# Moving the second latent pair's attention, gate, convolution and norm of layer 0 behind the first pair's router

## The reference

```
for l in range(2):
    hl, hc = modulated rmsnorm of latent and context tokens
    z = h @ w_in[l]        # q, k, v | mLSTM qk, v, o, gates | conv bg, cg, xv | 3 merge gates
    da = differential attention (latent queries see context + latent keys; context sees context)
    ml = mLSTM, both directions, chunks of 128 tokens
    cv = bg * conv3(cg * xv, w)                     # conv3 reaches one token to each side
    x += g1 * ((sig(gate0)*(da@w_da) + sig(gate1)*(ml@w_ml) + sig(gate2)*(cv@w_cv)) @ w_o)
    h = modulated rmsnorm(x)
    # PEER: 8 heads, each picks 16 of 16384 experts per token
    expert, gate = router(h)                        # 128 experts per token
    x += g2 * sum_k gate_k * gelu(u_tab[expert_k] . h) * v_tab[expert_k]
out = rmsnorm(latent x)
```

## Time and profile before

| | us |
|---|---|
| median of 3 runs | 5941.26 (5933.55 to 5946.65) |
| the profiled execution, whole | 5949.21 |
| its span | 5947.1 |
| b, from its first to c1's first matmul (762.2 to 1967.0) | 1204.8 |
| c1, to unit 3's last group (1967.0 to 2894.8) | 927.8 |
| c2, to d's first matmul (2894.8 to 3635.1) | 740.3 |
| e1, to unit 7's last group (4288.8 to 5260.7) | 971.9 |

### The profile page before, as it was taken

How to read it: one execution, slowest core, us unless ns; L and a number is a source line. 1 busy time by engine, 2 the same in 40 slices (tenths; PEclk the granted TensorE clock), 3 DMA queues, 4 the chain that set the end, 5 groups by cost and what they waited for, 6 DMA issues and landing times.

```text
span 5947.1 us, 63889 instructions
## 1 busy us (share of the span) xinstructions
PE 4117.5 (69%) x22248; PEld 2506.1 (42%) x22248; DVE 2900.9 (49%) x6835; ACT 1697.3 (29%) x4733; POOL 1441.5 (24%) x1295
## 2 busy tenths in 40 slices
PE   3889477889886685548476677778468785545555
PEld 1677454566563443224132235677335453211111
DVE  0321747544438544664445444322854445654444
ACT  0200137332432342233322222201152442222222
POOL 0000022212221232223343341000023332235443
PEclk7779789969997897778788888669778898767777
DMA  6434367748886798679999995024378997689998
GB/s 257 151 130 162 121 248 281 290 170 319 329 343 234 302 420 328 266 274 386 379 409 411 394 420 200 27 67 155 117 286 361 369 402 318 256 335 421 407 417 358
DMA packets 259315, 1712.65 MB, mean 288 GB/s; under 512 B 37712, under 2 KB 39344, under 8 KB 71600
## 3 DMA queue, kind: packets, MB, share of 16 engines
q0 software_dynamic: 184320, 1342.26, 56.4%
q1 hardware_dynamic: 74672, 366.31, 16.6%
HBM read 1690.43 MB, written 17.92 MB: 287 GB/s over the span
## 4 chain that ended last, share of the span: by engine, by line
PE 42%; DMA 24%; DVE 15%; ACT 6%; issue 4%; DVEq 4%; POOL 3%; ACTq 2%; SPq 1%; PEldq 0%; PEld 0%; POOLq 0%
PE psum L423 25%; DMA arena<-in_uv,arena 21%; PE psum L774 10%; DVE arena L2020 3%; POOL arena L1108 3%; DVE arena L1932 1%; DVE arena L1925 1%; DMA arena<-in_w_ada 1%; DVE arena L1926 1%; PE psum L383 1%; PE psum L604 1%; PE psum L605 1%; ACT arena L1444 1%; ACT arena L1441 1%; PE psum L639 1%
## 5 line engine op out<-in xcount | busy, mean ns | idle before, releaser
L1108 POOL DMA_INDIRECT arena<-in_uv,arena x1280 | 1437.6, 1123 | 4469.9 <-PE psum L774 3039.1
L774 PE MATMUL psum<-arena 64*64 64x512 f32 x10240 | 1564.5, 742 | 1086.5 <-ACTq L1445 990.9
L2020 DVE CUSTOM_DVE_ANT_0 arena<-arena 128x1024 f32<-128x1024 f32 x1280 | 1552.5, 1226 | 1330.0 <-DMA arena<-in_uv,arena 1272.4
L423 PE MATMUL psum<-arena 128*128 128x256 f32 (+2 forms) x8480 | 1945.9, 388 | 171.4 <-DVEq L1464 120.4
L423 PEld LDWEIGHTS psum<-arena 128*128 128x128 f32 (+1 forms) x8480 | 1616.9, 195 | 599.2 <-issue 194.1
L774 PEld LDWEIGHTS psum<-arena 64*64 64x64 f32 x10240 | 392.7, 157 | 2068.6 <-ACTq L1445 1375.8
L1438 ACT ACTIVATE arena<-arena 128x2 f32<-128x2 f32 x640 | 130.9, 205 | 1684.8 <-DVEq L2022 1671.3
L1444 ACT ACTIVATE arena<-arena 128x64 f32<-128x64 f32 x1280 | 376.2, 340 | 45.8 <-issue 1.8
L383 PE MATMUL psum<-arena 128*128 128x128 f32 (+1 forms) x680 | 129.4, 346 | 337.3 <-DVE arena L1523 119.8
L1441 ACT ACTIVATE arena<-arena 128x1 f32<-128x1 f32 x1280 | 307.6, 287 | 45.5 <-issue 1.3
L383 PEld LDWEIGHTS psum<-arena 128*128 128x128 f32 (+1 forms) x680 | 97.9, 178 | 391.2 <-issue 183.5
(11 more groups left out here) (210 smaller groups left out, 2747.4 us busy)
## 6 DMA issues: line engine op xcount, KB each, us to landing
arena<-in_w_in SPq DMA_DIRECT2D x92, 1024.0 KB, 5.9
arena<-in_w_mix SPq DMA_DIRECT2D x120, 768.0 KB, 7.3
arena<-in_w_ada SPq DMA_DIRECT2D x32, 1536.0 KB, 16.4
arena<-in_w_wq SPq DMA_DIRECT2D x40, 1152.0 KB, 6.0
arena<-in_w_wo SPq DMA_DIRECT2D x20, 1024.0 KB, 7.5
arena<-in_uv,arena POOLq DMA_INDIRECT x1280, 10.8
arena<-ada_rows SPq DMA_DIRECT2D x15, 512.0 KB, 5.6
arena<-x_rows SPq DMA_DIRECT2D x14, 512.0 KB, 6.2
```

The source lines that it names most:

```text
L423: ins = mm(out, a, b, start=(i == 0), stop=(i == last))
L774: ins = mm(psum[o, r_ * 512:r_ * 512 + 512], DIAG[rows, c, :], RING[rows, sl, D + half * 512:D + (half + 1) * 512], start=first, stop=last ...
L1108: pool.indirect_dma_start(RING[:, sl, :], None, io["uv"], bass.IndirectOffsetOnAxis(IDX[:, t, h * TOPK + k:h * TOPK + k + 1], 0)).then_inc ...
L2020: V_.tensor_tensor_reduce(out=RING[:, sl, 0:D], in0=RING[:, sl, 0:D], in1=XT[:, u % 2, :], scale=1.0, scalar=0.0, op0=ALU.mult, op1=ALU.ad ...
```

## The change

Segment b keeps `q`, `da` and `mc`, `mln` of pair 1 alone. Pair 2's `q`, `da`, `mc`, `mln` go to the head of c1, ahead of its `merge` and `route`. The four context stages of layer 1 go from c1 to the head of c2. b, c1 and c2 keep their numbers of groups, so the groups are spread anew over the steps.

What follows from it in the code: K^T and V (2 x 1.5 MB) are stored to DRAM (`kv_rows`) by SP at the head of `da` of pair 1, and loaded again at the first step of `q` of pair 2; ACT and DVE wait for the store at the head of `mlp`, and PE waits for the load ahead of pair 2's first scores. The weight chunks of `q` (2) and of `mc` (8) are loaded twice. Pair 1's convolution now goes ahead of pair 2's, so in its `mc` PE also multiplies the `cg` and `xv` chunks with pair 2's first column (64 matmuls of width 1, 128 instructions in the profile), and DVE finishes the last column from them. Some places in SBUF change.

```diff
-    b = [(k, 0, both) for k in ("norm1", "qkv", "da", "mlp", "ml", "mc", "mln")] + [("merge", 0, (1,)), ("route", 0, (1,))]
-    c1 = [("merge", 0, (2,)), ("route", 0, (2,))] + [(k, 1, (0,)) for k in ("norm1", "kv", "mlp", "ml")]
-    c2 = [(k, 1, (1,)) for k in ("norm1", "qkv", "mlp", "mc")]
+    b = [("norm1", 0, both), ("q", 0, (1,)), ("kv", 0, both), ("da", 0, (1,)), ("mlp", 0, both), ("ml", 0, both)] + [(k, 0, (1,)) for k in ("mc", "mln", "merge", "route")]
+    c1 = [(k, 0, (2,)) for k in ("q", "da", "mc", "mln", "merge", "route")]
+    c2 = [(k, 1, (0,)) for k in ("norm1", "kv", "mlp", "ml")] + [(k, 1, (1,)) for k in ("norm1", "qkv", "mlp", "mc")]
...
+                if (l, pairs) == (0, (2,)):
+                    pe.wait_ge(s("kv_in"), 32)
                 scores(0)
...
+                        if (l, pairs) == (0, (1,)) and name != "bg":
+                            after = buf(l, 2, "HT", [KD, PW])
+                            for i in range(2):
+                                (b,) = fill(("edge", l, name, 2 * hh + i))
+                                full(chain(bank(b, 1), [(w[:, k, i * P:(i + 1) * P], after[:, k, 0:1]) for k in range(KD)]))
...
+                        if (kind, l, pairs, n) == ("q", 0, (2,), 0):
+                            sp.wait_ge(s("kv_out"), 32)
+                            for i, a in enumerate((4096, 7168)):
+                                sp.dma_start(view(DN + a, [3072]), kv_rows[i]).then_inc(s("kv_in"), 16)
...
+                if (l, pairs) == (0, (1,)):
+                    for i, a in enumerate((4096, 7168)):
+                        sp.dma_start(kv_rows[i], view(DN + a, [3072])).then_inc(s("kv_out"), 16)
...
+                if (l, pairs) == (0, (1, 2)):
+                    dve.wait_ge(s("kv_out"), 32)
...
+                                if joined:
+                                    after = EDGE[:, m:m + 1]
+                                    (b,) = whole(("edge", l, "xv", m))
+                                    empty(TT(after, after, bank(b, 1), ALU.mult), b)
+                                    dve.drain()
+                                    conv_edge(cvt(p)[:, m, PW - 1:PW], HALO[:, 8 + m, :], after, CVCW[:, l, m, :])
```

More of the change, by code:

```diff
@@ L197, in build @@
         x_rows = nc.dram_tensor("x_rows", [TOK, D], fp32).ap()
+        kv_rows = nc.dram_tensor("kv_rows", [2, P, 3072], fp32).ap()
         def sem(name):
@@ L287, in build @@
                          RA=12288, RSM=14336, RW=8192),
-            (0, 2): dict(HT=2048, QT=11264, MLT=6144, MLV=9216, MLO=15872, CVT=7168, YMT=5120, YD=16384, YM=13312, G16=14080, STGQ=13312, STGK=15360,
-                         ROPE=16384, XS=12288, JUNK=14336, HST=15360, STAGE=12288, ROWS=14848, TEMPS=15360,
-                         COL=17920, CVS=16896, MT=8192, JUNK2=17408, SIG=12288, XS2=14336, G1=16384, RA=12288, RSM=14336, RW=8192),
+            (0, 2): dict(HT=2048, QT=10240, MLT=6144, MLV=9216, MLO=15872, CVT=7168, YMT=5120, YD=16384, YM=11264, G16=14080, STGQ=13312, STGK=15360,
+                         ROPE=0, XS=12288, JUNK=14336, HST=15360, E=12288, WM=13824, WT=14592, SQD=12288, STAGE=12288,
+                         SQM=8192, CVS=16896, NRD=18944, NRM=18944, MT=8192, JUNK2=17408, SIG=12288, XS2=14336, G1=16384, RA=12288, RSM=14336, RW=8192),
             (1, 0): dict(HT=2048, STGK=12288, XS=12288, JUNK=14336, HST=15360, MLT=15360, MLV=17408, STAGE=12288, G16=13824, ROWS=10240,
@@ L680, in edge @@
                     for i in range(2):
-                        (b,) = fill(("edge", name, 2 * hh + i))
+                        (b,) = fill(("edge", l, name, 2 * hh + i))
                         full(chain(bank(b, 1), [(w[:, k, i * P:(i + 1) * P], ht[:, k, 0:1]) for k in range(KD)]))
@@ L896, in qkv @@
             def qkv(kind, l, pairs):
-                for op in qkv_ops(kind):
+                for n, op in enumerate(qkv_ops(kind)):
                     for p in pairs:
@@ L1223, in mlp @@
             def mlp(kind, l, pairs):
+                if (l, pairs) == (0, (1, 2)):
+                    act.wait_ge(s("kv_out"), 32)
                 for p in pairs:
@@ L1529, in qkv @@
             def qkv(kind, l, pairs):
-                rope_at = DN + (1024 if kind == "q" else PLACE[l, pairs[0]].get("ROPE", 0))
+                rope_at = DN + (1024 if (kind, pairs) == ("q", (2,)) else PLACE[l, pairs[0]].get("ROPE", 0))
                 prods = [view(rope_at + 256 * i, [2 * H, 2, 16]) for i in range(4)]
@@ L1803, in mc @@
             def mc(kind, l, pairs):
+                joined = (l, pairs) == (0, (1,))
                 for c in range(2):
@@ L1821, in mc @@
                                 dve.drain().then_inc(s("cv_done"), 1)
+                                if joined:
[4 more added lines that the diff above has]
+                                    conv_edge(cvt(p)[:, m, PW - 1:PW], HALO[:, 8 + m, :], after, CVCW[:, l, m, :])
+                                    dve.drain()
+                            elif name == "cg" and joined:
+                                (b,) = whole(("edge", l, "cg", m))
+                                empty(V_.tensor_copy(EDGE[:, m:m + 1], bank(b, 1)), b)
                             elif name == "bg":
@@ L1824, in mc @@
                                 x = cvt(p)[:, m, :]
-                                if p == 1:
+                                if p == 1 and not joined:
                                     V_.tensor_copy(HBG[:, m:m + 1], bank(b)[:, PW - 1:PW])
@@ L1841, in edge @@
                         m = 2 * hh + i
-                        (b,) = whole(("edge", name, m))
+                        (b,) = whole(("edge", l, name, m))
                         e = EDGE[:, m:m + 1]
```

## The result

| | us |
|---|---|
| before, median of 8 runs | 5940.33 (5930.58 to 5949.73) |
| after, median of 8 runs | 5967.24 (5959.3 to 5980.9) |
| ratio, with its 95% interval | 1.0044 [1.0033, 1.0054] |
| span of the profiled execution, before and after | 5947.1, 5975.2 |

What follows compares the result with a forecast made beforehand. No one engine was taken to bound the kernel throughout: PE sets b's pace, gathers c2's, c1 lies between. Terms b -52, c1 +23, c2 +42 sum to +13 on 5941.3, forecast 5954 us, range 5905 to 6003.

Steps and rivals of the forecast that it cites:

- b: -52 forecast: Segment b as a whole: stages moved out, less the groups spread anew, were to shorten it by 52 us.
- priced at 27 by a row at half the clock: In `mc` of b: 128 width-1 instructions at 0.21 us each, taken from `edge`, 27.5 us with nothing hiding them.
- The third group's price of 10 us a head: In `route` of b: a third group delays the next head's scores; two heads pay 10 us each.
- The last head with 3 groups was given 5: In `route` of b: the last head with a third group pays only that group's own work, 5 us.
- e1 was the right row: For c1: e1 has nearly the stages c1 is to get; its 971.9 us was the base for c1's +23.
- the reload: At the head of c1: loading 3.1 MB delays unit 2's activations and what queues behind them, +5 us (bounds 0 and 16).
- half of one kind and half of the other: In c2: midway between +24 (bytes at 393 GB/s) and +59 (whole at 376 GB/s), giving 782 us, +42.
- the stretches taken as unchanged: Segments a, d, e1 and the end were to stay as they are, adding nothing to the sum.
- the gathers hide all of it: Rival, c1 and c2: moved steps fill idle transfer time, c1 stays at 928, c2 pays bytes; -28, 5913 us; chance 0.25.
- The two sides cancel: Rival, whole kernel: c2 pays bytes alone, c1 and b as forecast; -5, 5936 us; chance 0.17.
- The width-1 matmuls hide: Rival, `mc` of b: they hide in the groups' waits, the sum without its 27; -14, 5927 us; chance 0.05.
- the stops add up: Rival, c1 and c2: reload holds PE and stops gathers, c2's short stages run at 376 GB/s; +47, 5988 us; chance 0.13.

Runs made afterwards that it cites:

- route_two: The kernel after, with router cost 9.6 instead of 12 for pair 1 in layer 0, so every head has 2 groups: 5930.52 us, ratio 0.9983.
- no_width1: The kernel after, without the width-1 matmuls in pair 1's `mc` and the small VectorE operations that wait for them: 5949.41 us, ratio 1.0012.
- ctx_small_chunks: The kernel after, with the 8 weight chunks of the context's stages in c2 loaded at a sixteenth of their size: 5960.71 us, ratio 1.0037.

## Why the prediction was right, and where it was off

The sign and the mechanism held: b pays back less than was taken out of it, and the two stretches behind it don't take the work for nothing.

- b: -52 forecast, -50 measured. Of its stages, five came within 3 us of their forecast: `q` and `kv` 117 (117), `merge` 250.5 (252), `mln` 5.9 (about 9), `ml` 167.3 (169), `mc` 122.9 (123.5). `mlp` was 6 shorter than forecast, its 3 new groups cost next to nothing (142.5 for 142.0); `da` was 8 longer (92.8 for 85). Why, no run asks.
- `mc` was right by luck: two errors cancelled. The width-1 instructions were priced at 27 by a row at half the clock; they take 15. In turn the rest of the stage was priced 8 too low: 103.6 without them, not 96. The prediction says that the trace disagrees with the Trainium skill's page "TensorE: Matmul & The Clock Gate", section "LDWEIGHTS" (107 ns for 128 columns). At the full clock it agrees, 108 ns each. The loads fill the same time as the matmuls in the earlier trace rows, which points to the weight load as what is left at a width of 1. That such an instruction costs what one of width 256 does was wrong too: the one price was at half speed, the other at full speed.
- `route`: 229.2 for 224 forecast. The third group's price of 10 us a head is what route_two measured. The last head with 3 groups was given 5; the stage as a whole grew by 30 for its three.
- c1: +23 forecast, +21 measured; e1 was the right row, and the reload cost about the 5 us given to it.
- c2 is the term that was mis-sized: +42 forecast, +62 measured, 3 above even its upper bound. The prediction took the middle between the bytes' time at 393 GB/s and the rate of the context's stretch, 376. The step that failed is "half of one kind and half of the other". Pair 1's half did not keep its 393: it ran at 372, below the context's 383. One cause is shown. The change gave the 8 lead groups to the context's norm, and pair 1's got the stop of 24 us, which the row of c2 before does not have. Putting a lead back is worth 13 to 24 us.
- In all +27 for +13: 20 us too low in c2, less 5 from the stretches taken as unchanged. The forecast of the whole was about half of the loss.
- The rivals: "the gathers hide all of it" is out, as c1 is 949 long and not below 935. "The two sides cancel" had c2 at its bytes alone, +24. "The width-1 matmuls hide" is out by no_width1's 18 us. Of "the stops add up" half came true: c2's part (+59), but not the wait for the reload.

## What to carry to other kernels

Price a moved piece by what is spread around it anew: here the groups left behind in b took back about half of what the moved stages freed (`merge` +19 and `route` +30 among them), and a change of a cost table by one number was worth 37 us. Where an engine's stream has work that lags by a fixed number of items, count how many are handed out between two steps of a latency chain; one above the lag puts the chain's next link behind the current one. A lead of groups ahead of a stage that begins with a load covers the stop there; moving stages can take it away. Before taking a row as a price, read the granted clock of its stretch.

## What the runs showed of the hardware

The same 128 matmul instructions of width 1 take 27.5 us at a granted clock of 0.50 and 15.0 in a stretch whose mean is 0.86. `edge` was granted 0.50 in the mean, the lower level, although PE was busy in it for 27.5 of 28.9 us. It stands behind `mlp` of pair 2, which ran close to the full clock:

```profile
3635.10:3725.30 90.20, 83.75 (x392) 70.91 (x392) 33.35 (x95) 25.77 (x54) 0.00 (x0) 0.94 0.34 118
```

In `mc`, where steps of width 256 and groups stand between them, a step with these instructions had 1.00. Transfers reached 420 GB/s in single stages, for example here, `mlp` of pair 1 in c2 of the kernel after:

```profile
3383.20:3516.40 133.20, 102.42 (x576) 51.20 (x576) 67.91 (x124) 38.35 (x131) 53.21 (x46) 0.88 1.01 420
```

Leaving out 7.9 MB of weights beside gathers saved 7 us of c2, not the 19 that they take at 408 GB/s. In c2 POOL stood for 426 us in the kernel after and for 428 in ctx_small_chunks until PE had freed a slot: the gathers came at the pace of the slots, with or without the chunks.
